# Six attention slots issued from inside the last projection block, with tile 0's attention buffers moved to free places

## What is computed

```
z = h @ w_in                                   # h (tokens, 1024), w_in (1024, 2628)
dq, dk, dv, sq, sk, sv, iq, ik, iw = split(z)
# four differential heads
a = softmax(q1 k1 + bias) - lam * softmax(q2 k2 + bias)
o = rms_norm(a @ v, g_subln) * (1 - lam_init)
# eight sparse heads: the top keys by an indexer's score, then softmax attention with bias
p = softmax(where(selected, q k + bias, -inf));  o = p @ v
x = x + ga1 * rms_norm(o @ w_out, g_post_mix)
x = x + ga2 * rms_norm((silu(g) * u) @ w_down, g_post_ffn)
```

## Time and profile before

| | us |
|---|---|
| median of three runs | 1480.02 |
| the profiled execution's own time | 1478.52 |
| its span, first to last instruction | 1476.6 |
| PE busy | 1411.9 (96% of the span) |
| DVE busy | 1052.3 (71%) |
| ACT busy | 645.0 (44%) |
| POOL busy | 313.8 (21%) |
| last projection matmul's evacuation begins | 364.14 |
| first bias of tile 1 begins | 379.95 |

### The profile page before, as it was taken

The page is one execution under the profiler, slowest core; times in us unless marked ns, Lnnn a source line. Parts: engine busy times, 40 slices in busy tenths (PEclk is TensorE's granted clock), DMA queues, the critical chain, the costliest instruction groups (busy, mean ns, idle before and its releaser), DMA issues.

```text
span 1476.6 us, 26730 instructions
## 1 busy us (share of the span) xinstructions
PE 1411.9 (96%) x9519; PEld 1224.3 (83%) x9519; DVE 1052.3 (71%) x2308; ACT 645.0 (44%) x1362; POOL 313.8 (21%) x353
## 2 busy tenths in 40 slices
PE   5999999999899999989998999999999999999997
PEld 3776999998456666668878999999999999888876
DVE  4539999994799877764687666566656665875687
ACT  4546222222677677763663223323332332543353
POOL 3111211111111100001114344434433440000011
PEclk9999999999799999989999999999999999999999
DMA  9410556733555554522331332333233307995323
GB/s 295 135 51 14 150 185 196 235 95 100 117 153 160 157 145 118 154 87 86 115 115 45 117 115 82 105 88 115 72 115 115 106 25 264 310 313 184 110 87 142
DMA packets 180164, 198.28 MB, mean 134 GB/s; under 512 B 19773, under 2 KB 136830, under 8 KB 180074
## 3 DMA queue, kind: packets, MB, share of 16 engines
q1 hardware_dynamic: 180074, 197.11, 43.9%
HBM read 154.00 MB, written 43.08 MB: 133 GB/s over the span
## 4 chain that ended last, share of the span: by engine, by line
PE 87%; DVE 4%; ACT 3%; issue 2%; DMA 2%; SPq 1%; POOL 1%; DVEq 0%; POOLq 0%; ACTq 0%
PE PJ L2533 15%; PE S L2829 14%; PE S L2906 8%; PE T L2829 8%; PE PJ L2829 7%; PE S L2682 5%; PE PJ L2906 4%; PE T L2906 4%; PE S L2799 4%; PE PJ L2799 3%; PE T L2655 3%; PE PJ L2744 2%; PE PJ L2747 2%; PE S L2589 1%; PE S L2688 1%
## 5 line engine op out<-in xcount | busy, mean ns | idle before, releaser
L1803 DVE TENSOR_SCALAR_CACHE_REDUCE scrap<-work,cand 128x384 uint8<-128x384 f32 (+6 forms) x217 | 177.9, 884 | 1.1
L2533 PE MATMUL PJ<-hTh,wh 128*128 128x352 f32 (+2 forms) x480 | 162.0, 338 | 0.0
L2533 PE MATMUL PJ<-hTh,wl 128*128 128x352 f32 (+2 forms) x480 | 157.3, 328 | 0.0
L2533 PE MATMUL PJ<-hTl,wh 128*128 128x352 f32 (+2 forms) x480 | 157.3, 328 | 0.0
L670 POOL TENSOR_TENSOR wab_a<-graw,wab_a 128x512 fp32r<-128x512 f32 x63 | 87.5, 1402 | 246.8 <-ACT wab_a L1405 246.8
L2125 DVE TENSOR_TENSOR mix_later<-mix_later,S 128x256 f32<-128x256 f32 (+1 forms) x147 | 61.0, 427 | 65.9 <-PE S L2829 64.9
L1148 POOL TENSOR_TENSOR wl<-wraw,wh 128x1024 fp32r<-128x1024 f32 (+1 forms) x21 | 49.5, 2357 | 265.4 <-ACT wh L1237 265.4
L2829 PE MATMUL S<-tokA,wab_a 128*128 128x256 f32 x792 | 98.8, 283 | 0.6 <-ACT mix_later L1405 0.6
L2829 PEld LDWEIGHTS S<-tokA,wab_a 128*128 128x128 f32 x792 | 96.9, 191 | 0.9 <-issue 0.7
L2533 PEld LDWEIGHTS PJ<-hTh,wh 128*128 128x128 f32 (+1 forms) x480 | 90.4, 188 | 8.4 <-issue 6.8
L2533 PEld LDWEIGHTS PJ<-hTl,wh 128*128 128x128 f32 (+1 forms) x480 | 90.5, 189 | 0.3
(11 more groups left out here) (358 smaller groups left out, 3548.2 us busy)
## 6 DMA issues: line engine op xcount, KB each, us to landing
graw<-in_w_gu SPq DMA_DIRECT2D x44, 512.0 KB, 5.4
ada<-in_w_ada SPq DMA_DIRECT2D x16, 1024.0 KB, 7.5
draw<-in_w_down SPq DMA_DIRECT2D x55, 256.0 KB, 3.6
h_scratch<-hid SPq DMA_DIRECT2D x22, 544.0 KB, 3.4
s_scratch<-hsum SPq DMA_DIRECT2D x11, 1024.0 KB, 4.2
draw<-s_scratch SPq DMA_DIRECT2D x44, 256.0 KB, 3.9
wraw<-in_w_in SPq DMA_DIRECT2D x20, 512.0 KB, 5.8
draw<-h_scratch SPq DMA_DIRECT2D x33, 256.0 KB, 2.9
```

The costliest lines, as they stand in the source:

```text
L1803: return nc.vector.tensor_scalar(seen[0:r, 0:n], work[0:r, o:o + n], least_score, None, ALU.is_ge, ALU.add, accum_out=rows_at(count, i))
L2533: last = pe.matmul(chunk_bank(3 * b + c)[0:w, 0:n], wp[:, b % 2, k, 0:w], hp[:, k, c0:c0 + n], start=(k == 0 and p == 0), stop=(k == KB - ...
```

## The change

The slots 0 to 5 of attention are issued from inside the last projection block (block 20): an even slot ahead of each chunk, an odd one between the two halves of its matmuls. For this

- block 20's chunks collect in the upper halves of S[0] and S[1], while scores of tile 0 (128 columns) use the lower halves and the value products use PJ;
- tile 0's probabilities, turned probabilities and heads get buffers of their own (`sc_t0`, `aT_t0`, `ob_t0`, `obj_t0`), since the usual ones lie over `hTh`;
- SP loads tile 0's queries 0 to 3 and its values one block earlier, and its queries 4 to 6 ahead of the last block's store; tile 0's values leave the list behind the store;
- the transpose of the gates and the exponential of lambda come one block earlier; POOL clears e_first's corner one block earlier, and does the first two heads' root mean squares ahead of its wait for the last chunk.

The core of the diff (functions that only move up in PE's text, and ACT's and DVE's buffer names, are left out):

```diff
+UNDER_LAST = 6
...
+        sc_t0 = place("sc_t0", [128, 4, 2, 128], F32, 168448)
+        aT_t0 = place("aT_t0", [128, 2, 2, 128], F32, 185344)
+        ob_t0 = place("ob_t0", [128, 2, 128], F32, 189440)
+        obj_t0 = place("obj_t0", [128, 128], BF16, 190464)
...
         def chunk_bank(i):
 
+            if i >= 3 * (NB - 1):
+                return S[i % 2][:, 512:1024]
...
             for b in range(NB):
+                if b == NB - 2:
+
+                    sp.wait_ge(score_acc, NH_I * len(TOPK_TILES))
+                    for d in QBLOCKS[2:4]:
+                        sp.wait_ge(q_stored[q_slot[d]], 16 * (q_count[d] + 1))
+                    load_q(0, 0, 4)
+                    for s in range(2):
+                        sp.wait_ge(nat_stored[s], 32 * len([v for v in NATURAL if nat_slot[v] == s]))
+                    sp.wait_ge(ada_used, N_ADA)
+                    load_values(0)
                 if b == NB - 1:
 
-                    sp.wait_ge(score_acc, NH_I * len(TOPK_TILES))
                     sp.wait_ge(q_stored[q_slot[b - 1]], 16 * (q_count[b - 1] + 1))
                     sp.wait_ge(q_stored[q_slot[b - 2]], 16 * (q_count[b - 2] + 1))
-                    load_q(0, 0, 7)
+                    load_q(0, 4, 7)
                     load_q(1, 0, 7)
...
+            sp.wait_ge(ld_q7, 16)
             load_q(0, 7, 8)
             sp.wait_ge(ld_q[1], 16)
             load_q(1, 7, 8)
-            load_tile(0)
...
+            pool.wait_ge(chunk_done, 3 * 17)
+            pool.memset(e_first[0:64, :, 0:64], NEG).then_inc(corner_ready, 1)
+            head_rms(0)
+            head_rms(1)
             pool.wait_ge(chunk_done, 3 * NB)
-            pool.memset(e_first[0:64, :, 0:64], NEG).then_inc(corner_ready, 1)
             pool.memset(e_second[0:64, 0:13, 0:64], NEG).then_inc(corner_ready, 1)
+            head_rms(2)
+            head_rms(3)
...
+            for slot in range(UNDER_LAST):
+                head_slot(slot)
+                if slot in (2, 4):
+                    chunk_evac(NB - 1, slot // 2 - 1)
+            chunk_evac(NB - 1, 2)
+            for slot in range(UNDER_LAST, SLOTS):
+                head_slot(slot)
...
-            def chunk(b, c, between):
+            def chunk(b, c, between, slot=None):
...
                     if k == KB // 2:
                         for pair in between:
                             dots(*pair)
+                        if slot is not None:
+                            head_slot(slot)
                     chunk_rows(b, c, k)
...
-                if s >= 2:
+                if s < 2:
+                    pe.wait_ge(chunk_out, 3 * (NB - 1))
+                else:
                     wait_products_read(pe, s - 2)
...
+            for c in range(3):
+                head_slot(2 * c)
+                chunk(NB - 1, c, (), 2 * c + 1)
+            for slot in range(UNDER_LAST, SLOTS):
+                head_slot(slot)
```

More of the change, by code:

```diff
@@ L1185, in _ @@
                 s = behind(slot, VALUE_LAG)
[L1186 to L1188 removed]
+                if s is not None and s >= 8 and not sparse(s):
+                    head_rms(s)
             for t in range(NT):
@@ L1485, in equals_out, with head_slot @@
                              ).then_inc(freed(key), 1)
-            for slot in range(SLOTS):
+            def head_slot(slot):
                 s = behind(slot, TURN_LAG)
@@ L1514, in _ @@
                     split_out(k)
+            for b in range(NB - 1):
+                for c in range(4):
+                    for t, p in dots_pairs(b, 2 * c) + dots_pairs(b, 2 * c + 1) if c < 3 else dots_pairs(b, 6):
+                        r, n = rows_of(t), nkeys(t)
+                        for hh in range(2):
+                            u = NH_I * (t - 2) + 2 * p + hh
+                            act.wait_ge(dots_done, u + 1)
+                            if u >= 2:
+                                act.wait_ge(score_acc, u - 1)
+                            nc.scalar.activation(relu[0:r, u % 2, 0:n], S[u % 2][0:r, 0:n], ACT.Relu, scale=SCALE
+                                                 ).then_inc(relu_done, 1)
+                    if c < 3 and (b, c) not in FIRST_CHUNKS:
+                        chunk_evac(b, c)
+                    if b == NB - 2 and c == 1:
+                        act.wait_ge(lam_ready, 1)
+                        nc.scalar.activation(lam[:, 2:4], lam[:, 0:2], ACT.Exp).then_inc(lam_ready, 1)
+                    if c < 3 and b == 2:
+                        cache_out(c)
+                    for q in nat_groups(b, c):
+                        nat_out(b - 1, q)
+                if b and b + 2 < NB:
+                    split_w(b + 2)
+                for j in ada_after(b):
+                    row_out(j)
+            for slot in range(UNDER_LAST):
[5 more added lines that the diff above has]
+                head_slot(slot)
             def rows_turned(t):
@@ L2776, in _ @@
                         ranks(t, q, PJ[(slot + 1) % 2])
+            for b in range(NB - 1):
+                kind, _, _, w = BLOCKS[b]
+                if b == 3:
+                    pe.wait_ge(chunk_out, 9)
+                for c in range(4):
+                    for pair in dots_pairs(b, 2 * c):
+                        dots(*pair)
+                    if c < 3 and (b, c) not in FIRST_CHUNKS:
+                        chunk(b, c, dots_pairs(b, 2 * c + 1))
+                    if c < 3 and b == 2:
+                        turn_cache(c)
+                    for q in nat_groups(b, c):
+                        turn_block(b - 1, q)
+                for j in ada_after(b - 1)[1:]:
+                    ada_transposes(j, j)
+                for j in ada_after(b):
+                    if j == ADA_FIRST:
+                        pe.wait_ge(relu_done, NH_I * len(TOPK_TILES))
+                    ada_products(j)
+                for j in ada_after(b)[:1]:
+                    ada_transposes(j, j)
+            pe.wait_ge(gates_ready, 1)
+            bank = t_wait_free(pe, ("gates",))
+            pe.transpose(bank[0:32, 0:128], gates[:, :, :, :].rearrange("p a g k -> p (a g k)"), ident[:, :]
+                         ).then_inc(filled(("gates",)), 1)
+            for c in range(3):
[3 more added lines that the diff above has]
+                head_slot(slot)
             def out_products(t, half, ks):
```

94 lines of the change are left out of this document (29 added, 65 removed).

## The result

The kernel with the change takes **1482.91 us** (median of 12 runs), the kernel before beside it on the same chip 1478.89 us (12 runs): a ratio of **1.0027, 95% interval 1.0019 to 1.0036**, so 2.8 to 5.3 us slower. 1481.6 had been forecast, with 1478.8 to 1485.4 as the range.

A forecast was written before the change was run, and what follows sets the result against it. The prediction took the store and e_second's load to set the end, 15.81 us behind the projection. +2.5 - 0.95 - 0.3 + 0.3 = +1.6 us on 1480.02 gave 1481.6 us, range 1478.8 to 1485.4.

The forecast's parts named there:

- T': New end of the projection, where its last evacuation begins; forecast 2 to 3 us later than 364.14.
- G: Start of tile 1's first bias on DVE, 379.95 us in the kernel before, 15.81 us behind the projection's end.
- X: PE's work of slots 0 to 5 added inside the last block: +2.5 us, bounds 2.1 and 4.9.
- the transfer: e_second's load: 0.3 us gained without tile 0's 320 KB ahead, 0.3 us lost to tile 2's loads.
- the landing: Sign of a right forecast: e_second's second load lands 9.5 to 10 us after its issue.
- SP's list: Two issues of tile 0's values removed behind the store, so e_second is issued earlier: -0.95 us.
- 1 (slots stall the block): Rival: slots' rounds or late queries stop PE in the last block; +4.6 us, 1484.6; chance 0.17.
- 2 (tile 2's loads crowd the transfer): Rival: tile 2's earlier loads slow e_second's by 2 us, not 0.3; +3.3 us, 1483.3; chance 0.10.
- 3: Rival: e_second's load gains 1.5 us and the clock returns 3 us sooner; -0.6 us, 1479.4; chance 0.12.
- 4: Rival: slot 0 waits and slots bunch up behind the block; 1479.1; chance 0.06, shared with anything unseen.
- The clock: PE's clock at tile 1's start: taken as 0, with 1 us to either side; 0.2 us by the skill's rule.

The follow-up runs named there:

- loads_only: The change with no slot inside the last block, early loads and own buffers kept: 1477.64 us, ratio 0.9990 to the kernel before.
- strip_loads: strip_after with no slot inside the last projection block: 1477.09 us, ratio 0.9976 to the kernel before.
- strip_after: The change with e_second in four buffers in places free a block earlier, loaded in block 19: 1477.55 us, ratio 0.9985 to the kernel before.
- double: The change with the scores of slots 0 to 5 computed twice, the second overwriting the first: 1485.21 us (one run).
- slots2: The change with only slots 0 and 1 inside the last block: 1480.18 us, ratio 1.0003 to the kernel before.
- slots4: The change with only slots 0 to 3 inside the last block: 1479.75 us, ratio 1.0002 to the kernel before.
- filler_long: The change with 16 unused identity matmuls behind slot 6 and 34 behind slot 8: 1480.59 us, ratio 1.0004 to the kernel before.
- filler: The change with 16 unused identity matmuls behind slot 6 and 20 behind slot 8: 1481.05 us, ratio 1.0007 to the kernel before.
- strip_fill: strip_after with 16 unused identity matmuls behind slot 6: 1473.01 us, ratio 0.9957 to the kernel before.
- loads_fill2: strip_loads with unused identity matmuls behind tile 0's slots, 2 behind slots 0 to 2, 1 behind slots 3 to 6: 1472.18 us, ratio 0.9953 to the kernel before.

## Why the prediction was right, and where its sum was wrong

**The bound was right.** The end was set by the store and e_second's load; the six slots stood beneath them and came out on top. loads_only shows it from the one side (without slots T' to G is 13.9 all the same), strip_loads and strip_after from the other (with the load gone, it is the slots that T' to G measures: 12.92 without them in the block, 8.69 with them).

**The time was hit in part by luck.** 1481.6 is the median of three runs, 1480.02, and 1.6 us; the kernel before took 1478.89 beside the change, and 1479.15 to 1480.41 beside the other kernels. The step itself was forecast as +1.6 us and came out as +2.7 in the traces and +4.0 in the medians. It would have been further off if two errors had not gone against each other: X was 2.05 us too small, and the transfer gained 0.95 where nothing was taken. By the line of 0.2% that the prediction drew itself the outcome is "slower", which it gave 0.28, and not "same" with 0.64. Two of its signs were missed too, T' by 4.59 us later where 2 to 3 stood, and the landing 8.9 us after the issue where 9.5 to 10 stood. (With half a microsecond to each side its range would be 1478.9 to 1485.1, and holds the result as well.)

**The step that failed is X, the PE work of slots 0 to 5**: forecast 2.5 (2.1 to 4.9), measured 16.41 - 11.86 = **4.55 us**. By the rows of the chain after:

| | forecast | measured |
|---|---|---|
| scores | 1.74 | 6 x 0.42 = 2.52 |
| transposes | 0.33 | 3 x 0.26 = 0.78 |
| value products | 0.45 | 2 x 0.22 = 0.44 |
| block 20's own matmuls, longer behind each slot | 0 | 12.56 - 11.86 = 0.70 |
| the gates' transpose, moved ahead too | not counted | 0.11 |

The sentence that went wrong is "I take 2.5, since the transposes among chunks are the nearest case". Four transposes among chunks have the projection's shape of 128 rows, and add no more than their own work. The scores have 64 rows, and what was moved alternates between the two shapes twelve times. A nearer case stood in the same trace, the indexer's products of 64 rows between the halves of a chunk. The double run gives the group's own work, 0.22, less than the 0.29 forecast; with that the work itself is 1.32 + 0.33 + 0.44 = 2.1 us, the lower bound, and 4.55 - 2.1 - 0.11 = 2.3 us is left for leaving and coming back, 0.4 for each of six insertions. The upper bound of 4.9 ("each group its whole latency") held the value, and was the better guess.

**The other terms.** SP's list: -0.95 forecast, -0.95 measured. The transfer: -0.3 + 0.3 forecast, -0.95 measured; as far as one profile of the kernel before tells, tile 0's 320 KB had run ahead of it after all, and tile 2's loads, which go out 3.7 us behind the second load, did not hold it up. It landed 8.9 to 9.1 us after its issue in the change, loads_only, slots2, slots4, double and filler_long, whatever ran beside it, against 9.9 before; in filler's profile alone it took 10.3, for a reason that no run shows. Sum: 4.55 - 0.95 - 0.95 = 2.65, and 2.69 at G.

**The rivals.** 1 (slots stall the block) is false: PE has no gap in the block, DVE waits 1.2 to 2.0 us for each of the slots 1 to 5. 2 (tile 2's loads crowd the transfer) is false by the landing time. 3 is true in its first half (0.95 of the 1.5 us), not in its second: the clock came back at 394.8, 12 us behind G, where it had been 11. 4 is false: slot 0's scores stand right behind block 19 (352.39). The prediction gave "X near 4.9" a tenth of the forecast's chance, and that is what happened.

**The clock.** In the kernel after PE was granted the full clock to 374.3, half of it to 377.7, full to 381.1 and half again to about 394.8 (one row for each turn, in the same columns as above):

```profile
374.00:375.00 1.00, 0.94 (x6) 0.72 (x7) 0.29 (x3) 0.00 (x0) 0.00 (x0) 0.64 0.52 131
378.00:379.00 1.00, 0.40 (x5) 0.14 (x1) 0.00 (x0) 0.90 (x5) 0.90 (x2) 1.00 1.15 205
381.00:382.00 1.00, 0.00 (x0) 0.00 (x0) 0.00 (x0) 0.00 (x0) 0.00 (x0) 0.56 1.07 229
394.00:395.00 1.00, 1.00 (x6) 0.49 (x5) 0.77 (x4) 0.56 (x3) 0.11 (x1) 0.62 0.00 0
```

Slot 9 starts at half clock, where the clock fell at its start before, and from G on the two kernels take the same 270.2 us. So 0 was the right term for this change. The size beside it was not seen: tile 1 at half clock costs both kernels some 3 us, which strip_fill and loads_fill2 get back (first output product 266.8 and 267.3 us behind G). The Trainium skill (TensorE: Matmul & The Clock Gate, "Why this matters for your kernels") says to leave no idle gaps between bursts of matmuls. filler_long and strip_fill agree with it, with 2.3 and 2.8 thousandths off the kernels that they were made from. filler's median is 2.0 thousandths lower too, but its one profile lost the clock and gained nothing.

**What stays open** is the last microsecond: +2.7 us by the trace, +2.9 by the two profiled executions, +4.0 (2.8 to 5.3) by the medians. Single executions of one kernel differ by more: the change's by 5.5 us (1479.32 to 1484.84), and its four at a mean clock of 0.982 to 0.984 are 1479.3 to 1481.9, its seven at 0.978 to 0.980 1481.8 to 1484.8. A share of the slow stretches that varies, or a landing like filler's 10.3, would be enough, or the kernel before itself, whose medians beside the other kernels lie up to 1.5 us above the 1478.89. The slow stretches and the landing were not measured in the runs without a profile.

## What to carry to other kernels

Before work is moved to fill a gap elsewhere, ask what covers it now: six slots beneath a load cost nothing, the same slots in a block without a gap cost their whole time and the switching besides. Small groups of matmuls of another row count than their surroundings are priced by a case that alternates shapes, not by one that keeps them (here 0.4 us an insertion, as much as the work itself). Take the transfer off the path first, then see what the engines do in its place, the clock included; the order of the work mattered less here than both.

## What the runs showed of the hardware that was not expected

- A group of four score instructions (weights of 64 rows) takes 0.22 us behind its like and 0.42 behind projection matmuls of 128 rows, where it starts 0.25 us after the last of them in place of 0.16, its weights not loaded ahead. One insertion adds 0.62 us in all, four transposes of 128 rows between projection matmuls 0.44.
- Some 3.7 us of identity matmuls in one wait (32 instructions behind slot 6) were followed by full clock up to 402 us, and gave 4.9 us at the first output product over strip_after (295.8 against 290.9). In filler it fell behind 3.27 us without a matmul, in strip_loads behind three waits of 0.6 to 0.7 us among short slots.
- e_second's 1.3 MB landed 1 us sooner in six of seven profiles without the 320 KB issued ahead of it (8.9 to 9.1 us, 10.3 in the seventh) than in the one with them (9.9), and in those six no later for 832 KB issued behind it.
